# Second attention of a two-layer network on one core: turns moved into the projection, values in pieces, the norm after the output product

## The reference, cut to what matters

```python
h = rms_norm_2(x, g_mix_norm)
z = h @ w_in                                    # 1024 -> 2840
q, kc, vc, ks_, vs_, kw_, vw_, gl, hc, cg, bg = jnp.split(z, offs, axis=-1)
q = rms_norm_2(q.reshape(B, T, 8, 64), g_q)     # 8 heads in 2 groups
k_cmp = rms_norm_2(compress(kc, ...), g_k[0])   # blocks of 32 keys, stride 16, + pe, @ w_cmp1, gelu, @ w_cmp2
v_cmp = compress(vc, ...)
attn_out = nsa_attention(q, k_cmp, v_cmp, k_slc, v_slc, k_win, v_win, gates)
    # three softmax branches per head: compressed (31 blocks), selected, window;
    # with 512 tokens both latter ones see all earlier keys; distance bias slope * (t - s);
    # o = g0 * o_cmp + g1 * o_slc + g2 * o_win
conv_out = bg * causal_conv3(cg * hc)
mixed = concat([rms_norm_2(attn_out, g_out[:512]), rms_norm_2(conv_out, g_out[512:])])
x = x + mixed @ w_o
h = rms_norm_2(x, g_ffn_norm)
x = x + square(relu(h @ w_up)) @ w_down         # 1024 -> 4096 -> 1024
```

## Time and profile before

| | us |
|---|---|
| median of 3 runs | 2069.99 |
| profiled execution, its own time | 2061.46 |
| its span, first to last instruction | 2060.1 |
| TensorE busy | 1789.1 (87%) |
| VectorE busy | 847.5 (41%) |
| ScalarE busy | 530.3 (26%) |
| POOL busy | 136.4 (7%) |
| mean granted clock of TensorE | 0.958 of full speed |

### The profile page before, as it was taken

How to read it: one execution, slowest core, us unless ns; L and a number is a source line. 1 busy time by engine, 2 the same in 40 slices (tenths; PEclk the granted TensorE clock), 3 DMA queues, 4 the chain that set the end, 5 groups by cost and what they waited for, 6 DMA issues and landing times.

```text
span 2060.1 us, 20584 instructions
## 1 busy us (share of the span) xinstructions
PE 1789.1 (87%) x8329; PEld 1180.8 (57%) x8329; DVE 847.5 (41%) x1303; ACT 530.3 (26%) x881; POOL 136.4 (7%) x130
## 2 busy tenths in 40 slices
PE   3998889897888985788888888889988899999998
PEld 1657575775777863223233323377744478888876
DVE  4075372346753336011011111255676644444443
ACT  2134342333532323100000000123254432222221
POOL 0002030213000000100000000000100101001110
PEclk9999999998999998899999999999999799999999
DMA  9131201204014042699999999814320022322201
GB/s 341 58 123 41 82 21 65 79 5 160 1 42 170 1 163 82 278 422 422 422 421 421 421 422 421 329 54 150 82 82 1 1 82 82 116 89 82 85 38 41
DMA packets 92426, 329.40 MB, mean 160 GB/s; under 512 B 7421, under 2 KB 22701, under 8 KB 67757
## 3 DMA queue, kind: packets, MB, share of 16 engines
q1 hardware_dynamic: 84448, 312.59, 38.9%
q10 hardware_dynamic: 5932, 8.16, 1.2%
q0 software_dynamic: 1952, 7.34, 0.9%
HBM read 322.82 MB, written 4.19 MB: 159 GB/s over the span
## 4 chain that ended last, share of the span: by engine, by line
PE 65%; DMA 14%; DVE 12%; ACT 4%; issue 3%; ACTq 1%; POOL 1%; SPq 1%; DVEq 0%
PE PS L579 19%; PE PS L360 12%; PE PS L678 8%; PE PS L909 8%; DMA ring<-in_w_exp_down_dram 6%; DMA ring<-in_w_exp_gate_dram 5%; PE PS L356 3%; PE PS L548 3%; PE PS L689 2%; PE PS L744 2%; DVE wR L1444 1%; PE PS L440 1%; ACT wR L963 1%; DMA ring<-in_w_mod_dram 1%; PE PS L859 1%
## 5 line engine op out<-in xcount | busy, mean ns | idle before, releaser
L579 PE MATMUL PS<-hR,wR 128*128 128x512 f32 x1200 | 300.0, 408 | 29.3 <-DVE wR L1444 15.9
L579 PEld LDWEIGHTS PS<-hR,wR 128*128 128x128 f32 x1200 | 231.5, 195 | 95.4 <-issue 29.3
L678 PE MATMUL PS<-ring,xeT 128*64 128x512 f32 x1024 | 230.3, 600 | 40.2 <-DMA ring<-in_w_exp_gate_dram 37.9
L1444 DVE TENSOR_TENSOR wR<-ring,wR 128x1024 fp32r<-128x1024 f32 (+2 forms) x142 | 161.0, 1135 | 250.8 <-ACT wR L963 250.6
L963 ACT CAST wR<-ring 128x1024 fp32r<-128x1024 f32 (+2 forms) x142 | 138.3, 975 | 215.9 <-PE PS L909 126.8
L678 PEld LDWEIGHTS PS<-ring,xeT 128*64 128x64 f32 x1024 | 76.7, 138 | 192.5 <-issue 186.1
L909 PE MATMUL PS<-wR,hR 128*128 128x512 f32 x768 | 176.2, 390 | 8.9 <-DVE tmp L2123 6.9
L579 PE MATMUL PS<-xR,wR 128*128 128x512 f32 x768 | 175.3, 389 | 0.0
L909 PEld LDWEIGHTS PS<-wR,hR 128*128 128x128 f32 x768 | 143.6, 188 | 41.5 <-DVE tmp L2123 9.6
L579 PEld LDWEIGHTS PS<-xR,wR 128*128 128x128 f32 x768 | 144.1, 188 | 29.8
L678 PE MATMUL PS<-ring,hidT 128*64 128x512 f32 x512 | 116.6, 603 | 24.3 <-DMA ring<-in_w_exp_down_dram 18.4
(11 more groups left out here) (385 smaller groups left out, 2186.7 us busy)
## 6 DMA issues: line engine op xcount, KB each, us to landing
ring<-in_w_exp_gate_dram SPq DMA_DIRECT2D x64, 1024.0 KB, 13.7
ring<-in_w_exp_up_dram SPq DMA_DIRECT2D x64, 1024.0 KB, 13.7
ring<-in_w_exp_down_dram SPq DMA_DIRECT2D x64, 1024.0 KB, 12.9
ring<-in_w_mod_dram SPq DMA_DIRECT2D x12, 2048.0 KB, 9.2
ring<-in_w_in_dram SPq DMA_DIRECT2D x11, 2048.0 KB, 9.1
ring<-in_w_up_dram SPq DMA_DIRECT2D x8, 2048.0 KB, 8.4
ring<-in_w_down_dram SPq DMA_DIRECT2D x8, 2048.0 KB, 7.8
ring<-in_w_in_dram SPq DMA_DIRECT2D x9, 1024.0 KB, 5.3
```

Of the source, the lines that this page charges most:

```text
L579: mm = T.matmul(b, o[s][:, k, :], x[:, t, k, :], start=(k == ks[0] and j == 0), stop=(k == ks[-1] and j == 2))
L678: mm = T.matmul(b[es, ns], stat[:, 2 * kq + k, es], W.view(units[e2])[:, k, ns], start=(kq + k == 0), stop=(kq == 3 and k == 1))
L1444: V.tensor_tensor(lo, W.view(unit)[:, ks, cs], hi.bitcast(F32), ALU.subtract) \
```

## The change

- **Turns.** The turns of queries and keys move from the head of `select` to behind conv tiles 8 and 9 of the projection, their copies to ScalarE behind tiles 9 and 10, with the copy of the distance table. POOL's slopes start once the conv's taps are done.
- **Blocks and squares.** The eight adds that build `blkT` move from VectorE to POOL. The squares of `vc` are no longer taken by ScalarE and summed by four products, but squared and added up on POOL, and one product sums them over the partitions.
- **Order of the steps.** Scores 0 and 1 come ahead of the block product; the compress chain stands in steps 2 to 4, the compressed scores of the first block in step 5, their turn in step 7. The conv norm stands in steps 5 to 12 of VectorE's order, one tile a step, and its result is at once split into `hiC` (ScalarE) and `loC` (VectorE).
- **Values in pieces.** The output product is split by pairs of heads and by branch into four pieces of 256 columns, in steps 6, 7, 10 and 11 of a block, counted from its first; the compressed part comes as a fifth piece behind step 9. The output has bank 7 for itself, and the common pool shrinks to banks 4, 5 and 6.
- **Norm after the product.** The attention output is scaled by `g_out` and split unnormalized into `hiA` (ScalarE, four copies) and `loA` (VectorE, four operations) block by block. Each `w_o` tile is two half products, of the conv half and of the attention half, in two banks; VectorE multiplies the second by `rinv` while adding both to the residual. POOL's scaling and the eight splits at the start of `ffn` go. The first two weight chunks of `w_o` are split at the end of the steps, and the conv halves of tiles 0 and 1 are multiplied first.
- **Small ones.** The exponentials of the compressed scores run over 32 columns instead of 31; their mask product and their maximum with 1e-30 stay only for block 0.

The diff, cut to what the prediction speaks of:

```diff
+                    if key[1] == 8:
+                        T.wait_ge(*dve_sec["qn", 1])
+                        for i in range(4):
+                            b = pool.take(T, ("q2T", i), act_sec["q2T", i])
+                            for j in range(4):
+                                mm = turn(b[:, 128 * j:128 * j + 128], q2[:, i, 128 * j:128 * j + 128])
+                            mm.then_inc(pe_sec.sem, pe_sec.up(("q2T", i)))
+                    if key[1] == 9:
+                        for v, src in enumerate((ksw, kww)):
+                            b = pool.take(T, ("k2T", v), act_sec["k2T", v])
+                            for i in range(4):
+                                mm = turn(b[:, 128 * i:128 * i + 128], src[:, i, 0:128])
+                            mm.then_inc(pe_sec.sem, pe_sec.up(("k2T", v)))
...
+            pool, four, last = Banks(4, 7), Banks(0, 4), Banks(7, 8)
+            T.wait_ge(*act_sec["k2T", 1])
...
+            def conv_sum():
+                b = pool.take(T, "vc2", dve_sel["vc2"])
+                T.wait_ge(*pool_sec["vc2"])
+                T.matmul(b, ones, sq[:, 0, :], start=True, stop=True).then_inc(pe_sel.sem, pe_sel.up("vc2"))
...
+            def values2(i, jp, v):
+                m = 8 * (3 - i) + 4 * jp + 3
+                b = bank(("o2", i))
+                if jp + v == 0:
+                    b = last.take(T, ("o2", i), dve_sel["mx", i])
+                T.wait_ge(*act_sel["pT", m - 1 + v, 1 - v])
+                if v:
+                    T.wait_ge(*dve_sel["pT", m, 1])
+                vt = (ksw, kww)[v]
+                for c in range(i + 1):
+                    for g in range(2):
+                        mm = T.matmul(b[64 * g:64 * g + 64, 256 * jp:256 * jp + 256], vt[:, c, 128 + 64 * g:192 + 64 * g],
+                                      pT2[v][:, c, g, 2 * jp:2 * jp + 2].rearrange("p j q -> p (j q)"),
+                                      start=(jp + v + c == 0), stop=(jp + v == 2 and c == i))
+                mm.then_inc(pe_sel.sem, pe_sel.up(("o", i, jp, v)))
...
+            def compressed3(i, jp):
+                b = bank(("o2", i))
+                if jp == 0:
+                    T.wait_ge(*dve_sel["cpT", i])
...
+            def mixed(n, half):
+
+                key = ffn_chunks[n][0]
+                b = pool.take(T, (*key, half), dve_ffn["w", key[1], half])
+                T.wait_ge(*dve_lo[key])
+                T.wait_ge(*dve_sel[("conv", 3) if half else ("mx", 0)])
+                o = parts(wR3, ffn_chunks, n)
+                for k in range(4):
+                    for j, (s, t) in enumerate(TERMS):
+                        mm = T.matmul(b, o[s][:, 4 * half + k, :], mix_parts[t][half][:, k, :], start=(k + j == 0),
+                                      stop=(k == 3 and j == 2))
+                mm.then_inc(pe_mm.sem, pe_mm.up((key, half)))
+                if half == 0:
+                    pe_mm.also((key, 0))
...
+                    if t != 1:
+                        mixed(n, 1)
+                    if t == 0:
+                        mixed(1, 1)
+                    mixed(n, 0)
...
+        for m in range(38):
+            i = 3 - m // 8
             if m < 32:
                 scores(m)
-            if m < 3:
-                (compress1, compress2, compress3)[m]()
-            if m >= 3 and (m - 3) % 8 == 7:
-                values2(m - 3)
+            if m == 1:
+                blocks()
+            if m == 2:
+                compress1()
+                conv_sum()
+            if m == 3:
+                compress2()
+            if m == 4:
+                compress3()
+            if 6 <= m < 36 and (m - 6) % 4 < 2:
+                block, part = divmod(m - 6, 8)
+                values2(3 - block, part // 4, part % 4)
             if 2 <= m < 34:
                 turn2(m - 2)
-            if m < 32 and m % 8 == (3 if m < 8 else 1):
-                compressed1(sel_steps[m][0])
-            if m < 32 and m % 8 == (6 if m < 8 else 5):
-                compressed2(sel_steps[m][0])
-            if m >= 4 and (m - 4) % 8 == 7:
-                square2(sel_steps[m - 4][0])
+            if m < 32 and m % 8 == (5 if m < 8 else 1):
+                compressed1(i)
+            if m < 32 and m % 8 == (7 if m < 8 else 5):
+                compressed2(i)
+            if m in (9, 17, 25, 33):
+                compressed3(i + 1, 0)
+                compressed3(i + 1, 1)
+            if m in (13, 21, 29, 37):
+                square2(i + 1)
+            if conv and m in (5, 6, 7, 8, 9, 10, 11, 12):
+                conv(m - 5)
...
+            def values2(i, jp, v):
+                if i == 0 and jp + v == 2:
+                    A.wait_ge(*pe_sel["pT", 31, 1])
+                    A.wait_ge(*s.last)
+                    copy_hi(wR3, ffn_chunks, 0)
                     A.wait_ge(*dve_sel["tot", 1])
                     A.activation(rinv[:, 128:512], rinv[:, 128:512], ACT.Sqrt).then_inc(s.sem, s.up(("rms2", 1)))
+                if jp + v == 2:
+                    A.wait_ge(*pe_sel["o", i, 1, 1])
+                    if i < 2:
+                        A.wait_ge(*pe_sel["tot", i + 2])
+                    else:
+                        A.wait_ge(*pe_sel["vc2"])
+                    A.activation(sq[:, i % 2, :], bank(("o2", i)), ACT.Square).then_inc(s.sem, s.up(("sqa", i)))
+                    for j in range(4):
+                        A.activation(hiA[:, j, 128 * i:128 * i + 128], bank(("o2", i))[:, 128 * j:128 * j + 128], ACT.Copy,
...
+            def conv(n):
+                if n == 0:
+                    V.wait_ge(*act_sel["rinv"])
+                    V.reciprocal(rinv, rinv).then_inc(s.sem, s.up())
+                    V.wait_ge(*s.last)
+                if n < 4:
+                    V.scalar_tensor_tensor(vc[:, n, :], vc[:, n, :], colA[:, 52 + n:53 + n], rinv, ALU.mult, ALU.mult) \
+                        .then_inc(s.sem, s.up(("conv_n", n)))
+                else:
+                    V.wait_ge(*act_sel["conv", n - 4])
+                    V.tensor_tensor(loC[:, n - 4, :], vc[:, n - 4, :], hiC[:, n - 4, :].bitcast(F32), ALU.subtract) \
+                        .then_inc(s.sem, s.up(("conv", n - 4)))
 
...
+                if jp + v == 2:
+                    V.wait_ge(*act_sel["hiA", i, 3])
+                    for j in range(4):
+                        qs = slice(128 * i, 128 * i + 128)
+                        V.scalar_tensor_tensor(loA[:, j, qs], bank(("o2", i))[:, 128 * j:128 * j + 128],
+                                               colA[:, 48 + j:49 + j], hiA[:, j, qs].bitcast(F32), ALU.mult, ALU.subtract) \
+                            .then_inc(s.sem, s.up(("mx", i) if j == 3 else None))
...
+                    part = tmp[:, t % 4, :]
+                    V.wait_ge(*pe_mm[key, 1])
+                    V.tensor_tensor(xT[:, t, :], xT[:, t, :], bank((*key, 1))[:, 0:512], ALU.add) \
+                        .then_inc(s.sem, s.up(("w", t, 1)))
                     V.wait_ge(*pe_mm[key, 0])
-                    V.tensor_tensor(xT[:, t, :], xT[:, t, :], bank(key)[:, 0:512], ALU.add).then_inc(s.sem, s.up(("x4", t)))
+                    V.tensor_tensor(part, bank((*key, 0))[:, 0:512], rinv, ALU.mult).then_inc(s.sem, s.up(("w", t, 0)))
+                    V.wait_ge(*s.last)
+                    V.tensor_tensor(xT[:, t, :], xT[:, t, :], part, ALU.add).then_inc(s.sem, s.up(("x4", t)))
...
+        for g in (pe_mm[("conv", 11), 0], act_sec.end, dve_sec.end):
+            G.wait_ge(*g)
+        G.wait_ge(s_sh, 128)
+        for v in range(2):
+            for g in range(2):
+                source = shA[:, 2 * v + g, :].rearrange("p (i l) -> p i l", l=16)
+                for half in range(2):
+                    src = source[:, half:half + 31, :].rearrange("p i (l u) -> p l u i", u=2)[:, :, 0, :]
+                    pe_ = colB[:, 32 + 16 * v + 8 * half:40 + 16 * v + 8 * half]
+                    G.tensor_tensor(blkT[:, 8 * half:8 * half + 8, v, g, 0:31], src,
+                                    pe_.unsqueeze(2).broadcast_to([128, 8, 31]), ALU.add).then_inc(pool_sec.sem, pool_sec.up())
+        G.memset(blkT[:, :, :, :, 31:32], 0.0).then_inc(pool_sec.sem, pool_sec.up("blk"))
+        G.tensor_tensor(sq[:, 0, :], vc[:, 0, :], vc[:, 0, :], ALU.mult).then_inc(pool_sec.sem, pool_sec.up())
+        for k in range(1, 4):
+            G.wait_ge(*pool_sec.last)
+            G.tensor_tensor(sq[:, 1, :], vc[:, k, :], vc[:, k, :], ALU.mult).then_inc(pool_sec.sem, pool_sec.up())
+            G.wait_ge(*pool_sec.last)
+            G.tensor_tensor(sq[:, 0, :], sq[:, 0, :], sq[:, 1, :], ALU.add).then_inc(pool_sec.sem, pool_sec.up())
+        pool_sec.also("vc2")
         for r in range(8):
```

266 lines of the change are left out of this document (105 added, 161 removed).

## The result

The changed kernel takes 2090.85 us (median of 4, 2087.66 to 2093.24) beside 2069.99 for the kernel before: a ratio of 1.0106, interval 1.0077 to 1.0135. It is slower by about 21 us. The forecast was 2068, in a range that ended at 2081; rival B, the slower one, gave 2077 and is not what happened either.

A forecast was written before the change was run, and what follows sets the result against it. No engine was full in the steps: TensorE's in-order queue and VectorE's dependent chain held it. Terms -4.9 + 6.2 + 4.4 + 2.7 - 6.4 + 0.7 = +2.7 us gave 2064.2, raised to 2068; range 2048 to 2081.

The forecast's parts named there:

- rival B: Opening: POOL's adds and squares, slowed beside VectorE, delay the block product and compress chain; 8 to 10 us more, 2077; chance 0.20.
- the ring of three banks: Steps: compressed scores wait for ScalarE to empty a bank; 1.7 us in steps 5 to 7, 1.5 in block 1.
- The walk: Steps 8 to 15: queues followed with earlier trace durations; 37.6 us against 34.0, plus 0.8 for VectorE's late entry.
- the pieces: Steps 8 on: splitting the value product removes VectorE's idle time, 5.0 to 6.6 us, then about 5 and 3 later.
- Opening: Last conv tile to step 5: conv tiles end 3.0 us later, yet step 5 starts at 1514.1 instead of 1519.0, gain 4.9.
- Steps 5 to 7: Conv norm work now stands in VectorE's queue and a bank wait is added: 15.8 us becomes 22, loss 6.2.
- Steps 8 on: Steps 8 to 15 lose 4.4 us, steps 16 to 31 lose 2.7, the last turn coming at 1630.6.
- Tail: Into the feed-forward: tile 2 starts 22.4 us after the last turn instead of 28.3; gain 6.4, less 0.7 at the last tile.
- Footing: Whole time: 2064.2 on the profiled execution, moved up 4.5 us to the executions' middle, half a microsecond taken off: 2068.
- A: Steps 8 to 31: waits vanish in VectorE's backlog, so its own work sets the pace; 16 us less, 2052; chance 0.24.
- C: Steps: ScalarE's copies come earlier, so the three banks don't bind; 1.5 a block back, 2062; chance 0.13 together with D.
- D: Tail: it stays at 2.4 GHz and tile 2 isn't late; 4 us less, 2064; chance 0.13 together with C.

The follow-up runs named there:

- experiment 3: Changed kernel with each block's value product in one place again, still three common banks and a separate output bank; 2097.2 us, ratio 1.0127.
- experiment 2: Changed kernel with each block's value product in one place again and its output taken from a common pool of four banks; 2077.3 us, ratio 1.0042.
- experiment 4: Kernel before the change with only its common pool cut to three banks and a block's output given a bank of its own; 2085.04 us, ratio 1.0078.
- experiment 6: Changed kernel with the attention and feed-forward tiles moved 128 bytes, to multiples of 256, same instructions; 2085.86 us.
- experiment 5: Changed kernel with the input of gelu put in bank 7 instead of the common three banks; 2088.7 us, ratio 1.0092.
- Experiment 9: Changed kernel with one-piece value product, four banks, sum of squares in step 11, aligned feed-forward operands, conv norm back under the block product; 2063.39 us, ratio 0.9973.
- experiment 7: Kernel before the change, same order, with split weights, low part of x and temporaries at the changed kernel's addresses; 2073.74 us, ratio 1.0020.
- experiment 11: Kernel before the change with only the projection's operands moved 128 bytes, to multiples of 256; 2071.21 us, ratio 1.0009.
- experiments 10: Experiment 9's kernel with the projection's operands also moved 128 bytes, to multiples of 256; 2061.69 us, ratio 0.9965.

## Why the prediction was wrong

The step that failed is the price of the ring of three banks. The walk saw the ring, named a wait and its place, and put 1.7 us on it in steps 5 to 7 and about 1.5 a block behind them, some 6 in all; ahead of step 5 it put nothing. Taken away by itself the fourth bank costs 13.6 us in the changed kernel (experiment 3 against 2): 6.8 in the opening, where the walk had nothing, 2.1 in steps 5 to 7, and 5.8 in steps 8 to 24, where it had 3.0. In the old kernel it costs 10.6 to 13.0 in steps 8 to 24 (experiment 4). The 13.6 and the 6 us of the addresses, which no term of the sum had, make 20 of the 21 us. That is an estimate, as the pieces were never run with four banks.

The waits were near what was written: 6.0 us in four of them. Missing was what stands behind them. The walk moved on behind each wait with durations from the earlier trace rows, nearly all of them at the full clock, and experiment 4's matmuls took 7.9 to 10.0 us longer in steps 8 to 24 for about 3 us of added idle time. The prediction did quote the fall of the clock behind gaps, and used it for the tail and for the block product only. How much of the slow matmuls a wait brings isn't settled: in the changed kernel the ring adds only 3.7 us of busy time there (58.9 against 55.2), and from step 8 to the last turn one execution of the old steps has 7.5 us more of it than another, with no added wait.

A second term failed beside it, the pieces. The walk had them give back VectorE's idle time in each block, 5.0 to 6.6 us in steps 8 to 15 and about 5 and 3 behind, less their own place. The kernel after differs from experiment 3 in the pieces only, and in steps 8 to 24 it takes 75.6 us (73.8 in experiment 6) against 70.5. There the pieces cost 3 to 5 us. Over the whole stretch from the fourth conv tile to the turns of x the two are level, so the gain isn't in the runs.

*Opening.* Gain 3.1 instead of 7.9. The block product and POOL were right to 1 us, and so rival B fell: the sum on POOL ended at t+15.8. The compress chain was late because of the ring: a bank held until gelu (3.5 of waiting) and the bank of the sum of squares (3.2). I didn't see them because I followed the ring from the compressed scores on and not from its first taker. The ring costs 6.8 here by experiment 3; experiment 5 gives 3.5 to 6.3 for gelu's bank. With four banks (experiment 2) the stretch takes 30.8, a gain of 9.9.

*Steps 5 to 7.* Right: 5.4 against 6.2, of which the ring is 2.1 against 1.7. Experiment 9 bears out what they say, that the conv norm had cover under the block product and lost it.

*Steps 8 on.* Steps 8 to 16 lost 8.1, forecast 4.4; from step 16 on 8.4, forecast 2.7, but there the old steps themselves spread from 52.6 to 59.7 us between executions.

*Tail.* Tile 2 at 23.2 against 22.4; right in its parts. Of the 5.1 us gained there 1.7 are lost behind it, 0.7 forecast.

*Projection.* 4.3 against 3.0; of the same old order the three other profiles (experiments 4, 7 and 11) have 42.0 instead of 40.3, so the moved turns cost 2.6 to 4.3. Right within that.

*Rounds.* They weren't in the sum. Of their 7.7 us the addresses are 5.8 to 6.1 (experiments 6 and 7). The diff shows the move (`m11` from HT to DYN + 7264); no row of before could price it.

*Footing.* The sum started from an execution 8.5 us below the median, and I moved it up by 4.5. Experiments 7 and 11 took 261.7 and 258.0 from the fourth conv tile to the turns of x, where the profile of before has 253.7, so much of the low value was in just the stages that the change touches.

Rivals: A would have needed 24 steps under 80 us; they took 102.9. C had it the wrong way round: the ring binds, and costs more than forecast. D: no row of the tail shows it. Of the listed signs the ones on waits, on steps 8 to 15 and on the first half tile (last turn to its start 7.2 us, 5 forecast) held in kind; step 5 came 3.1 us earlier from the end of the projection, not 7.9. What stays open: what sets the granted clock of a sparse stage from one execution to the next, and so how much of the slow matmuls a wait brings.

The Trainium skill, page "TensorE: Matmul & The Clock Gate", section "HAM oscillation", was cited for D only. It says that idle gaps put the array back to half clock, and it would have been better used against the walk. This case's traces agree with it in part: the old steps with three banks have 0.74, the same steps with four have 0.88, 0.85 and 0.80 in three executions; but behind one and the same gap of 3.52 us a score takes 2.08 in the kernel after and 1.13 in experiment 6.

## What to carry to other kernels

In a stage where TensorE has gaps, don't price a new wait by its own length alone: in steps 8 to 24 of the old kernel three banks added 3 us of idle time, and the stage took 10.6 to 13.0 us more. Take the stage from several executions, since the clock of such a stage differs between them without any change. Before a shared pool of PSUM banks loses a bank, follow it from its first taker and ask of each who empties the bank and what is queued ahead of that copy; and before work is moved off a place where it looks idle, look what covered it there. When buffers get new addresses, compare one unchanged product in both traces.

## What the runs showed of the hardware

A down product whose split weights begin 128 bytes off a multiple of 256 takes 22.54 to 22.63 us for 96 matmuls, and 22.01 to 22.05 aligned, in both kernels and in either direction: 2.4%. Its weights are the moving operand; in experiment 7 they alone of its operands are off. An up product, in which the weights are loaded and the activations move, takes 21.99 to 22.02 instead of 21.77 when its weights and the low part of its activations are off. The two together make the 6 us over eight rounds. In the projection's products, also with loaded weights and moving activations, the same shift of both by 128 bytes brought nothing that can be told (experiments 10 and 11). Why the up product answers and these do not wasn't tried and stays open.

The granted clock of a sparse stage isn't the same in each execution of the same instructions: step 24 to the last turn of the old order ran at 0.78 in 24.5 us (before and experiment 11) and at 0.61 in 30.4 us (experiment 7), with 4.4 us of idle time in each.
